# Two instructions in place of sixteen: GpSimd's splitting of the output weights, block by block

## The chip, the cores and the metric

The kernel runs on one core of one Trainium2 chip. What counts is the time of one execution on the device in microseconds (us), as a median over runs.

## The reference

Two layers of a diffusion backbone over 1024 latent tokens and 256 context tokens, with a model width of 1024. Each layer normalises, modulates, projects in, mixes the tokens, gates, projects out with a 1024 x 1024 matrix, normalises again and adds the result to its input. Layer 0 mixes with dense attention and with an RWKV scan side by side, layer 1 with windowed attention. Cut to what matters here:

```python
def _even_mixer(hx, hc, ..., w_in, w_out, ...):
    ...
    oa_x = _dense_attention(qx, jnp.concatenate([kx, kc], axis=1), jnp.concatenate([vx, vc], axis=1))
    ...
    out_x = jnp.concatenate([oa_x * jax.nn.silu(gax), ob_x * jax.nn.silu(gbx)], axis=-1) @ w_out

def _odd_mixer(hx, hc, ..., w_in, w_out, ...):
    ...
    ox = _window_attention(qx, kx, _heads(vx, C_KV_HEADS), kc, vc, sink)
    out_x = (ox * jax.nn.silu(gx)) @ w_out
```

## The kernel before

The program is a row of stages with a barrier of all engines between them: modulation, input projection, decay streams, the chunked scan, dense attention, closing of layer 0, then input projection, window attention and closing of layer 1. All data is float32; matmuls of a projection are done as three products of a high half and a low half. The high half of a weight is its value rounded to the type fp32r, the low half is what the rounding left.

The output projection's weight is split into these halves one stage early, in `attention`, on GpSimd (POOL), which has nothing else to do there but some memsets at the start. `prepare` hands over the weight `w` in device memory and the two targets `w_hi` and `w_lo`, each 128 partitions x 8 x 1024. The weight comes in four blocks of 256 columns (`BLK`), through one buffer `w_raw` of 128 x 8 x 256 (`KC` is 8). For each block POOL waits until the buffer is free (L1765), issues the load of 1 MB from its own queue (L1766), waits for it (L1767), rounds (L1769) and subtracts (L1772). The first block waits until the first result tile of attention is done (`out_done`, L1763). The next stage, `closing`, is the first to read `w_hi` and `w_lo`, on TensorE (PE).

Attention itself goes by units. A unit is one tile of 128 queries by one group of four heads. In dense attention there are 20 units, in window attention 32. PE works in steps, one tile of 128 keys each. In a step it computes the turned scores (L1920 to L1925), perhaps one piece of the plain scores (L1892 to L1901), whose largest value is wanted ahead of the exponential, and the products with V (L1939). VectorE (DVE) does for a unit, in this order in its queue:

- L1814, `highest`: one reduce over the score piece in PSUM for each piece, four or eight a unit. The scores have one buffer, so PE's next piece waits for this reduce (`topped`).
- `turn`, after the last piece: the negated maximum (L1824 in window attention; L1827, or L1829 and L1831, in dense attention), then L1833, which multiplies the identity by it into `shift`, 128 x 512, and in window attention L1838, `sd`. Here these instructions are called the unit's chain.
- L1850 and L1854, `finish`: the division by the row sums.

Two steps after a unit's last piece PE spreads `shift` over the partitions (L1906); ScalarE (ACT) copies it into QM (L1786), and computes the exponentials (L1782).

Of the kernel before, what the change touches and what calls it, by code (L numbers as in the profile page):

```python
# [14 lines left out]
F32 = mybir.dt.float32  # L15
F32R = mybir.dt.float32r
ALU = mybir.AluOpType
# [12 lines left out]
KC = D // P  # L30
# [1586 lines left out]
def attention(nc, name, qst, kst, vrows, consts, orows, ngroups, units, edge=None, sink=None, prepare=None):  # L1617
# [40 lines left out]
    with Stage(nc, name) as st:  # L1658
# [25 lines left out]
        if prepare:  # L1684
            w, w_hi, w_lo = prepare
            w_raw = st.sb("w_raw", [P, KC, BLK])
            w_in, w_high, w_low = st.sems("w_in", "w_high", "w_low")
# [13 lines left out]
        with nc.Block() as block:  # L1701
# [42 lines left out]
            @block.gpsimd  # L1744
            def _(pool):
                pool.wait_ge(loaded, 16 * NCONST)
                pool.tensor_copy(ones_r[:], ones[:]).then_inc(rounded, 1)
                pool.wait_ge(rounded, 1)
                if window:
                    pool.tensor_copy(eye[:], ident[:]).then_inc(rounded, 1)  # L1750
                    pool.wait_ge(rounded, 2)
                    pool.tensor_copy(masks[:], masks_raw[:]).then_inc(rounded, 1)
                    pool.wait_ge(rounded, 3)
                pool.memset(KL[HD:P].rearrange("p g n -> p (g n)").bitcast(F32), 0.0).then_inc(filled, 1)
                pool.wait_ge(filled, 1)
                pool.memset(KL[HD:HD + 1].rearrange("p g n -> p (g n)").bitcast(F32), 1.0).then_inc(filled, 1)
                pool.wait_ge(filled, 2)
                pool.memset(V[:, :, :, HD:HW], 1.0).then_inc(filled, 1)
                pool.wait_ge(filled, 3)
                for b in range(D // BLK if prepare else 0):  # L1760
                    cols = slice(b * BLK, (b + 1) * BLK)
                    if b == 0:
                        pool.wait_ge(out_done, 1)  # L1763
                    if b >= 1:
                        pool.wait_ge(w_low, b * KC)  # L1765
                    pool.dma_start(w_raw[:], w.rearrange("(k p) n -> p k n", p=P)[:, :, cols]).then_inc(w_in, 16)  # L1766
                    pool.wait_ge(w_in, b * 16 + 16)  # L1767
                    for k in range(KC):
                        pool.tensor_copy(w_hi[:, k, cols], w_raw[:, k]).then_inc(w_high, 1)  # L1769
                    for k in range(KC):  # L1770
                        pool.wait_ge(w_high, b * KC + k + 1)
                        pool.tensor_tensor(w_lo[:, k, cols], w_raw[:, k], w_hi[:, k, cols].bitcast(F32), ALU.subtract).then_inc(w_low, 1)  # L1772

            @block.scalar
            def _(act):
# [90 lines left out]
            def _(pe):  # L1866
# [10 lines left out]
                def measure(i, q):  # L1877
                    u, s, g = units[i], i % NSLOT, units[i]["group"]
                    r, x = q // spans[i], q % spans[i]
                    width = len(tiles_of[i]) * P // spans[i] // 2  # L1880
                    lhs = Q[:, s, r * P:(r + 1) * P]
                    if q == 0:
                        pe.wait_ge(k_in[g], 16)
                        pe.wait_ge(q_in[s], (i // NSLOT + 1) * 16)
                    if window:
                        kts = [kt for kt, _ in u["edges"]]
                        wide = len(kts) * P
                        step = (kts[-1] - kts[0]) if len(kts) > 1 else 1
                        edges = K[:, g].rearrange("p (t n) -> p t n", n=P)[:, kts[0]:kts[-1] + 1:step]
                        to = score[:, 0, 0:wide].rearrange("p (t n) -> p t n", n=P)  # L1890
                        which = [w for _, w in u["edges"]]
                        pe.matmul(to, lhs, edges, start=True, stop=False)  # L1892
                        pe.matmul(to, eye[:], masks[:, which[0]:which[-1] + 1], start=False, stop=True)
                        mid, ctx0 = u["plain"][0] * P, u["plain"][1] * P
                        pe.matmul(score[:, 0, wide:width], lhs, K[:, g, ctx0:ctx0 + width - wide], start=True, stop=True)
                        pe.matmul(score[:, 1, 0:P], lhs, K[:, g, mid:mid + P], start=True, stop=True)
                        last = pe.matmul(score[:, 1, P:width], lhs, K[:, g, ctx0 + width - wide:ctx0 + 2 * P], start=True, stop=True)  # L1897
                    else:
                        for b in range(2):
                            c0 = u["plain"][0] * P + (x * 2 + b) * width  # L1900
                            last = pe.matmul(score[:, b, 0:width], lhs, K[:, g, c0:c0 + width], start=True, stop=True)  # L1901
                    last.then_inc(scored, 1)
# [478 lines left out]
```

## Time and profile before

| what | value |
|---|---|
| median of three runs | 2652.66 us (2643.16 to 2656.72) |
| the profiled execution | 2652.66 us |
| its span, first to last instruction | 2650.9 us |
| mean granted TensorE clock | 0.907 of full speed |
| busy: PE, weight loads, DVE, ACT, POOL | 83%, 69%, 47%, 31%, 26% |
| instructions on POOL | 736 |

The busy share is the share of the span in which an engine executes an instruction, averaged over stages that have different limits. The granted clock is what the clock gate gave TensorE: 1.00 is 2.4 GHz and 0.50 is 1.2 GHz. A duration on DVE or POOL includes the time for which the instruction is held up after its start.

### The profile page before, as it was taken

To read this page: it belongs to the slowest core of one execution; us is meant where nothing else is said; L and a number is where in the kernel's file an instruction comes from. 1 tells how busy PE (TensorE), PEld (TensorE's weight loads), DVE (VectorE), ACT (ScalarE), POOL (GpSimd) and SP (SyncE) were. 2 spreads that over 40 slices of the span, in tenths; PEclk is the share of its full clock that TensorE was granted. 3 is DMA by queue.
4 is the path that set the end of the run, shared out by engine and by line. 5 is a ranking of instruction groups with operands and counts; after the bars stand their busy time and mean duration, and the time that the engine had idled before them with its cause. 6 is when DMAs were issued, how large, how long until landed. Compare 5 with 4: busy or idle time off the path is not lost. (4 is left out here: it accounts for less than half of the span.)

```text
span 2650.9 us, 59737 instructions
## 1 busy us (share of the span) xinstructions
PE 2188.2 (83%) x26094; PEld 1832.5 (69%) x26094; DVE 1256.8 (47%) x1692; ACT 825.7 (31%) x1393; POOL 694.9 (26%) x736
## 2 busy tenths in 40 slices
PE   4699999766558888888599998695799969999988
PEld 1588878622247777777488887574687758888866
DVE  1544553169725444454334442893546524444422
ACT  1311232155324444444123332221334302333321
POOL 0322463100023332323031000252357623200002
PEclk8799999877769999999779998797799978999989
DMA  6232333277632222221311110754344443211152
GB/s 219 93 108 85 94 96 105 62 257 278 252 108 80 63 85 62 87 70 38 85 64 48 41 33 30 226 162 161 117 110 105 120 116 109 65 56 48 38 196 88
DMA packets 232090, 282.38 MB, mean 107 GB/s; under 512 B 59796, under 2 KB 174676, under 8 KB 230804
## 3 DMA queue, kind: packets, MB, share of 16 engines
q1 hardware_dynamic: 204808, 194.28, 24.1%
q0 software_dynamic: 20688, 81.58, 9.1%
q8 instruction: 208, 3.41, 0.5%
q10 hardware_dynamic: 6336, 2.70, 0.4%
q14 instruction: 50, 0.41, 0.1%
HBM read 190.54 MB, written 87.95 MB: 105 GB/s over the span
## 5 line engine op out<-in xcount | busy, mean ns | idle before, releaser
L216 PE MATMUL in_acc<-in_hi,in_whi 128*128 128x512 f32 (+1 forms) x1024 | 392.2, 383 | 20.8 <-DVE in_lo L579 17.2
L216 PE MATMUL in_acc<-in_lo,in_whi 128*128 128x512 f32 (+1 forms) x1024 | 376.0, 367 | 0.0
L216 PE MATMUL in_acc<-in_hi,in_wlo 128*128 128x512 f32 (+1 forms) x1024 | 375.7, 367 | 0.0
L216 PEld LDWEIGHTS in_acc<-in_hi,in_whi 128*128 128x128 f32 x1024 | 196.2, 192 | 59.5 <-issue 28.3
L216 PEld LDWEIGHTS in_acc<-in_lo,in_whi 128*128 128x128 f32 x1024 | 196.6, 192 | 37.0 <-issue 7.2
L216 PEld LDWEIGHTS in_acc<-in_hi,in_wlo 128*128 128x128 f32 x1024 | 196.1, 191 | 31.8
L1814 DVE TENSOR_REDUCE dense_top<-dense_score 128x1 f32<-128x640 f32 (+1 forms) x144 | 112.3, 780 | 189.6 <-PE dense_score L1901 189.6
L1814 DVE TENSOR_REDUCE window_top<-window_score 128x1 f32<-128x640 f32 (+1 forms) x128 | 101.2, 791 | 190.5 <-PE window_score L1897 190.5
L1939 PEld LDWEIGHTS dense_outs<-dense_V,dense_p 128*128 128x128 f32 x1344 | 185.8, 205 | 5.0 <-ACT dense_p L1782 0.4
L1939 PE MATMUL dense_outs<-dense_V,dense_p 128*128 128x65 f32 x1344 | 182.0, 282 | 0.0
L1939 PE MATMUL window_outs<-window_V,window_p 128*128 128x65 f32 x1216 | 158.0, 274 | 0.2 <-ACT window_p L1782 0.2
L1939 PEld LDWEIGHTS window_outs<-window_V,window_p 128*128 128x128 f32 x1216 | 155.0, 195 | 4.0 <-ACT window_p L1782 0.6
L1468 PE MATMUL scan_wide<-scan_XT,scan_Y 64*64 64x64 f32 x3200 | 121.1, 224 | 24.1 <-issue 24.1
L1335 DVE TENSOR_TENSOR scan_X<-scan_X,scan_small 128x512 f32<-128x512 f32 x80 | 55.0, 687 | 180.9 <-PE scan_small L1463 179.7
L1782 ACT ACTIVATE dense_p<-dense_turned 128x512 f32<-128x512 f32 x168 | 96.6, 597 | 122.9 <-PE dense_turned L1925 122.4
L216 PE MATMUL close_acc<-w_hi,close_hi 128*128 128x512 f32 x288 | 117.6, 408 | 18.4 <-DVE close_lo L2187 18.4
L2113 POOL MEMSET close_eps<- 128x1 f32 x2 | 0.2, 104 | 496.7 <-POOLq L127 496.7
L1444 PE MATMUL scan_small<-scan_X,scan_off 64*64 64x64 f32 x3200 | 117.7, 225 | 8.2 <-issue 7.2
L1468 PEld LDWEIGHTS scan_wide<-scan_XT,scan_Y 64*64 64x64 f32 x3200 | 107.1, 136 | 24.7 <-issue 24.6
L1222 POOL TENSOR_TENSOR scan_off<-scan_LA,scan_lmask 128x512 f32<-128x512 f32 x100 | 124.0, 1275 | 0.0
L1213 POOL TENSOR_TENSOR scan_DG<-scan_LB,scan_lmask 128x512 f32<-128x512 f32 x20 | 25.3, 1265 | 364.3 <-ACT scan_LB L1249 364.3
L1444 PEld LDWEIGHTS scan_small<-scan_X,scan_off 64*64 64x64 f32 x3200 | 108.2, 140 | 14.0 <-issue 12.9
(256 smaller groups left out, 5038.6 us busy)
## 6 DMA issues: line engine op xcount, KB each, us to landing
streams<-decay_out POOLq DMA_DIRECT2D x8, 2560.0 KB, 13.1
scan_L<-streams SPq DMA_DIRECT2D x80, 256.0 KB, 3.6
decay_wm<-in_w_mod SPq DMA_DIRECT2D x16, 1024.0 KB
in_raw<-in_w_in_even SPq DMA_DIRECT2D x28, 512.0 KB, 3.7
in_raw<-in_w_in_odd SPq DMA_DIRECT2D x20, 512.0 KB, 3.9
close_ga<-gates SPq DMA_DIRECT2D x18, 512.0 KB, 4.5
modulation_w<-in_w_mod SPq DMA_DIRECT2D x4, 2048.0 KB, 15.4
gates<-in_outs POOLq DMA_DIRECT2D x32, 256.0 KB, 2.3
```

What stands on the lines that cost most here:

```text
L216: last = pe.matmul(out, a(k), b(k), start=(k == 0 and x == 0), stop=(k == n - 1 and x == 2))
L1213: pool.tensor_tensor(DG[:], LB[:], lmask[:, 0:1, :].to_broadcast([P, NU, HD]), ALU.mult).then_inc(diagonal, 1)
L1222: pool.tensor_tensor(off[s][:, k], triangles, lmask[:, k + 1:k + 2, :].to_broadcast([P, NU, HD]), ALU.mult).then_inc(off_done, 1)
L1335: dve.tensor_tensor(X[s][:], X[s][:], small[s][:], ALU.subtract).then_inc(x_less[s], 1)
L1444: return pe.matmul(small[s][half_of(1 - c), u, :], off[s][half_of(c), k, u, :], X[s][half_of(c), u, :], start=True, stop=True)
L1468: return pe.matmul(wide[s][half_of(1 - c), u, :], Y[s][half_of(1 - c), u, :], XT[j % 3][half_of(1 - c), u, :], start=True, stop=True)
L1782: act.activation(p[:, s % NP_], turned[s % NTURN][:], ACT.Exp, scale=SCALE).then_inc(expd, 1)
L1814: dve.tensor_reduce(top[:, i % NSLOT, x, r:r + 1], score[:, :, 0:width], AXS, ALU.max).then_inc(topped, 1)
L1939: last = pe.matmul(outs[i % 2][:, r * HW:(r + 1) * HW], p[:, s % NP_, r * P:(r + 1) * P], v, start=(k == 0 and r == 0), stop=(k == n - 1 a ...
L2113: pool.memset(eps[:, 0:1], EPS).then_inc(readied, 1)
```

## The change

Each block's eight casts of 256 columns become one cast of the whole block, and its eight subtractions one subtraction. The semaphores `w_high` and `w_low` count one for each block, not eight. The loads, the buffer and the order of the blocks stay.

```diff
                     if b >= 1:
-                        pool.wait_ge(w_low, b * KC)
+                        pool.wait_ge(w_low, b)
                     pool.dma_start(w_raw[:], w.rearrange("(k p) n -> p k n", p=P)[:, :, cols]).then_inc(w_in, 16)
                     pool.wait_ge(w_in, b * 16 + 16)
-                    for k in range(KC):
-                        pool.tensor_copy(w_hi[:, k, cols], w_raw[:, k]).then_inc(w_high, 1)
-                    for k in range(KC):
-                        pool.wait_ge(w_high, b * KC + k + 1)
-                        pool.tensor_tensor(w_lo[:, k, cols], w_raw[:, k], w_hi[:, k, cols].bitcast(F32), ALU.subtract).then_inc(w_low, 1)
+                    pool.tensor_copy(w_hi[:, :, cols], w_raw[:]).then_inc(w_high, 1)
+                    pool.wait_ge(w_high, b + 1)
+                    pool.tensor_tensor(w_lo[:, :, cols], w_raw[:], w_hi[:, :, cols].bitcast(F32), ALU.subtract).then_inc(w_low, 1)
```

## Rows read from the trace of the kernel before

**Rows 1.** Stretches: length, busy time (instructions) of each engine, granted clock, DMA share, GB/s

```profile
2218.00:2278.00 60.00, 54.38 (x396) 50.14 (x396) 29.14 (x56) 18.38 (x38) 36.88 (x67) 1.00 0.32 101
```

**Rows 2.** Waits in 1320 to 1690 us: who waited for whom, total, times, longest

```profile
POOL close_eps L2113 <- POOLq L127: 240.5, 1, 240.5
```

**Rows 3.** Timeline of POOL, dense attention: start, length, instruction, count

```profile
1355.14 2.80 POOL L1769 CAST w_hi<-dense_w_raw 128x256 fp32r<-128x256 f32 x8 [6.28 <-DMA dense_w_raw<-in_w_out_even]
1357.91 5.96 POOL L1772 TENSOR_TENSOR w_lo<-dense_w_raw,w_hi 128x256 fp32r<-128x256 f32 x8
...
1385.57 3.26 POOL L1769 CAST w_hi<-dense_w_raw 128x256 fp32r<-128x256 f32 x8 [5.50 <-DMA dense_w_raw<-in_w_out_even]
```

**Rows 4.** Timeline of POOL, window attention

```profile
2220.80 2.80 POOL L1769 CAST w_hi<-window_w_raw 128x256 fp32r<-128x256 f32 x8 [7.18 <-DMA window_w_raw<-in_w_out_odd]
2223.57 5.55 POOL L1772 TENSOR_TENSOR w_lo<-window_w_raw,w_hi 128x256 fp32r<-128x256 f32 x8
...
2235.99 2.80 POOL L1769 CAST w_hi<-window_w_raw 128x256 fp32r<-128x256 f32 x8 [5.63 <-DMA window_w_raw<-in_w_out_odd]
2238.75 6.00 POOL L1772 TENSOR_TENSOR w_lo<-window_w_raw,w_hi 128x256 fp32r<-128x256 f32 x8
...
2252.60 2.80 POOL L1769 CAST w_hi<-window_w_raw 128x256 fp32r<-128x256 f32 x8 [6.65 <-DMA window_w_raw<-in_w_out_odd]
2255.37 5.54 POOL L1772 TENSOR_TENSOR w_lo<-window_w_raw,w_hi 128x256 fp32r<-128x256 f32 x8
...
2267.72 2.81 POOL L1769 CAST w_hi<-window_w_raw 128x256 fp32r<-128x256 f32 x8 [5.62 <-DMA window_w_raw<-in_w_out_odd]
2270.49 5.98 POOL L1772 TENSOR_TENSOR w_lo<-window_w_raw,w_hi 128x256 fp32r<-128x256 f32 x8
```

**Rows 5.** Groups of POOL by form: busy us, mean ns of one, idle before

```profile
L472 POOL TENSOR_TENSOR in_work<-in_work,in_shift 128x1024 f32<-128x1024 f32 x20 | 47.9, 2394 | 76.9 <-DVE in_work L573 76.9
...
L503 POOL TENSOR_TENSOR in_work<-in_work,in_hu 128x512 f32<-128x512 f32 x30 | 38.7, 1291 | 7.5 <-DVE in_hu L614 7.5
...
L1752 POOL CAST window_masks<-window_masks_raw 128x256 fp32r<-128x256 f32 x1 | 0.4, 400 | 0.1
L1750 POOL CAST window_eye<-window_ident 128x128 fp32r<-128x128 f32 x1 | 0.3, 294 | 0.1
```

**Rows 6.** Timeline of DVE, dense attention

```profile
1359.36 0.66 DVE L1827 TENSOR_SCALAR dense_ntop<-dense_top 128x4 fp32r<-128x4 f32 x1
...
1387.03 0.33 DVE L1829 TENSOR_SCALAR dense_top<-dense_top 128x4 f32<-128x4 f32 x1
```

**Rows 7.** Timeline of DVE, window attention

```profile
2240.72 0.16 DVE L1824 SCALAR_TENSOR_TENSOR window_ntop<-window_top,window_nsinks_up 128x4 fp32r<-128x4 f32 x1
...
2251.66 0.16 DVE L1824 SCALAR_TENSOR_TENSOR window_ntop<-window_top,window_nsinks_up 128x4 fp32r<-128x4 f32 x1
...
2252.47 0.15 DVE L1838 TENSOR_TENSOR window_sd<-window_ntop,window_sinks_up 128x4 f32<-128x4 f32 x1
...
2262.22 0.16 DVE L1824 SCALAR_TENSOR_TENSOR window_ntop<-window_top,window_nsinks_up 128x4 fp32r<-128x4 f32 x1
...
2271.35 0.57 DVE L1824 SCALAR_TENSOR_TENSOR window_ntop<-window_top,window_nsinks_up 128x4 fp32r<-128x4 f32 x1
2271.96 1.19 DVE L1833 TENSOR_TENSOR window_shift<-window_ident,window_ntop 128x512 fp32r<-128x512 f32 x1
2273.07 0.68 DVE L1838 TENSOR_TENSOR window_sd<-window_ntop,window_sinks_up 128x4 f32<-128x4 f32 x1
```

**Rows 8.** Line L1833: count, shortest, median and longest in ns, first and last start

```profile
L1833 DVE TENSOR_TENSOR window_shift<-window_ident,window_ntop x32: 691/691/1191, 2180.8 to 2514.8; 128x512 fp32r<-128x512 f32 x32
```

**Rows 9.** Timeline of PE, window attention, at the only wait of this kind

```profile
2274.55 0.39 PE L1892 MATMUL window_score<-window_K,window_Q 128*128 128x256 f32 x1 [0.39 <-DVE window_top L1814]
```

**Rows 10.** Stretches of dense attention, columns as in rows 1

```profile
1440.00:1445.00 5.00, 3.61 (x24) 2.96 (x22) 1.42 (x4) 1.83 (x4) 0.00 (x0) 1.00 0.00 0
...
1445.50:1458.50 13.00, 12.08 (x48) 11.01 (x48) 3.76 (x6) 2.27 (x4) 0.00 (x0) 0.50 0.00 1
...
1470.00:1530.00 60.00, 55.70 (x395) 51.29 (x394) 28.29 (x48) 21.21 (x37) 0.00 (x0) 1.00 0.12 36
```

## The prediction

> **What bounds the kernel now.** The changed lines run only inside the two attention stages, so I look there first. The table of stretches shows what limits window attention while POOL splits the weight: PE is busy for 54.38 of 60 us, DVE for 29.14, POOL for 36.88 [rows 1]. PE sets the pace, and a microsecond in which PE waits is lost. Dense attention has the same picture with POOL idle: PE 55.70 of 60 [rows 10].
>
> Next I ask who waits for POOL. In the list of waits of dense attention POOL's own next work comes after 240.5 us of idling at the stage's end [rows 2]; the halves are read only in the stage after that. So whatever POOL saves here is not on the path. A first answer would be: no change.
>
> The third view is the timeline of DVE beside that of POOL, because a change of instruction length can act on a neighbour. L1833 takes 691 ns in the median but at most 1191 [rows 8], and the three instructions of the chain at 2271.35 took 0.57, 1.19 and 0.68 us [rows 7], where 0.16, 0.69 and 0.15 are usual [rows 7, 8]. All three lie within POOL's subtractions of 2270.49 to 2276.47 [rows 4]. The chain at 2251.66, when POOL was waiting for its load, has no such excess. So DVE is held up by a POOL instruction, each time by no more than about 0.5 us, which fits a wait until the POOL instruction under way (5.5 us over 8 is 0.7 us) has ended. In dense attention L1827 at 1359.36 took 0.66 [rows 6], also within POOL's subtractions [rows 3].
>
> What does such a wait cost PE? The chain at 2271.35 was held for 0.41 + 0.50 + 0.53 = 1.44 us, and shortly after it PE waited 0.39 us for DVE's maximum at 2274.55 [rows 9]. Hence a chain has about 1.44 - 0.39 = 1.05 us of slack, and what exceeds it stalls PE one for one.
>
> **The change part by part.**
>
> *Cast.* 294 ns for 128 columns, 400 for 256 [rows 5]: 0.83 ns a column. For the block's 8 x 256 = 2048 columns that is 400 + 1792 x 0.83 = 1.9 us in place of 2.80. The upper bound is the 2.80 of now, if nothing is saved.
>
> *Subtraction.* 1291 ns for 512 columns, 2394 for 1024 [rows 5]: 2.15 ns a column, and 2394 + 1024 x 2.15 = 4.6 us for 2048, in place of 5.5 to 6.0 [rows 4]. The upper bound again is the present time.
> Seen by itself: the Trainium skill, GPSIMD Engine Reference, section on elementwise work side by side, gives 4497 ns for a two-input add of 2048 columns. By it each subtraction would end 0.1 us sooner, and each wait below would be 0.1 us shorter, 0.2 us in the sum.
>
> A block then takes 6.5 us and not 8.3 to 8.8. POOL has about 2 us less work a block, eight blocks in all, some 16 us. That is hidden by the idling of [rows 2] and worth 0. The four loads of each stage start up to 6 us sooner; POOL issues the same DMAs from the same queue, no other instruction stands behind them, and DVE does not read what they bring. I cost that at 0, too.
>
> *The longer instruction.* POOL is now inside one instruction for 4.6 us at a stretch, where it had boundaries every 0.7 us at which DVE could get in. If DVE waits for the end of the instruction under way, a chain that falls into a subtraction waits up to 4.6 us, not 0.5. I place the new subtractions by keeping POOL's gaps between blocks (load and waits). Window attention [rows 4]:
> - block 0: cast from 2220.80, end 2227.3.
> - block 1: the gap is 2235.99 - 2229.12 = 6.9, so cast from 2234.2, subtraction 2236.1 to 2240.7. The chain at 2240.72 [rows 7] just escapes.
> - block 2: gap 2252.60 - 2244.75 = 7.85, cast from 2248.55, subtraction 2250.45 to 2255.05. The chain at 2251.66 is caught and waits 3.4 us; PE stalls 3.4 - 1.05 = 2.3 us.
> - block 3: gap 2267.72 - 2260.91 = 6.8, cast from 2261.9, subtraction 2263.8 to 2268.4. The chain of 2262.22, now 2.3 later at 2264.5, is caught and waits 3.9; PE stalls 2.8 us.
> - the chain of 2271.35 is free, and its 0.39 us of PE stall goes away.
>
> Sum for window attention: 2.3 + 2.8 - 0.4 = +4.7 us.
>
> Dense attention [rows 3, 6]: block 0's subtraction would lie at 1357.0 to 1361.6, the chain at 1359.36 waits 2.3 us, 1.2 over the slack. Its present two waits cost PE nothing, and PE's steps are longer there, so I take 0 and keep 1.2 for the range. Block 2 starts two savings of about 2 us sooner than 1385.57: subtraction 1383.4 to 1388.0, so the chain at 1387.03 waits 1.0, within the slack: 0.
>
> The sum is +4.7 us on the profiled execution of 2652.66, which is also the median: 2657.
>
> How firm is it? A wait is known from the rows only up to about 0.5 us; beyond that I assume that the wait grows with the POOL instruction. From below, the wait could stay at half a microsecond: then the sum is 0, or -0.4. From above, all eight subtractions could catch a chain at their start: 8 x (4.6 - 1.05) = +28 us. Chains come every 10.9 us (2240.72, 2251.66) and POOL subtracts for 4.6 us in about 14, so a chain is caught one time in three. I take my placed value, since the two catches in window attention have 1.2 us and 0.7 us of room before they would be missed.
> Seen by itself: the Trainium skill, SBUF — State Buffer, section on who interferes with whom, speaks against this change. It says that DVE and GpSimd share one pair of ports as an exclusive lock, held for the whole instruction by whichever came first, and that a DVE instruction with two SBUF inputs contends with a GpSimd instruction that reads SBUF. The short waits agree; no row yet shows a long one. By the rule the sum is the +4.7 above, by a wait capped at what the rows show it is -0.4.
>
> **The rivals.**
>
> *R1, nothing happens.* The wait does not grow, or the chains miss the subtractions because the loads land at other moments, or the merged instructions are no quicker than the eight they replace (the gain per instruction is not real; the engine would then only show other boundaries). For it: the catches hang on placements good to half a microsecond. Against it: every chain inside POOL work shows an excess now. Time: 2652 to 2653.
>
> *R2, the clock falls (slower).* PE at 1440 to 1445 was busy for only 3.61 of 5 us, and from 1445.5 to 1458.5 the granted clock was 0.50 (1.2 GHz) [rows 10]. In that stretch PE issued 48 matmuls in 13 us, 3.7 per us, against 395 in 60 us, 6.6 per us, at 1.00: it cost 13 x (1 - 3.7/6.6) = 5.7 us. A stall of 2.3 or 2.8 us leaves PE as idle or idler than before that fall. One such stretch added gives 2657.4 + 5.7 = 2663, two give 2669. It decides the sign beyond my bound from the second stretch on, or with one that lasts over 20 us. Against it: window attention ran at 1.00 throughout [rows 1], with margin unknown.
>
> *R3, faster.* The low stretches of dense attention move, and some fall away, as the waits of DVE shift. Each is worth 5.7 us by the same row; three would be needed to show. What speaks for it is only that the present runs differ by 13 us among themselves. Time: below 2639.
>
> **How the numbers follow.** What a measurement of this kernel can tell from no change is about 0.5%, 13.3 us. Chances: my forecast, one to three chains caught and no low stretch added, 2657 (2653 to 2662), 0.50. R1, 2652, 0.22. R2 with one added stretch, 2663, 0.12; with two or more, over 2666, 0.12. R3, 0.04. So faster 0.04, same 0.50 + 0.22 + 0.12 = 0.84, slower 0.12. The range leaves out the last two of these, 0.16: its lower end is the lowest of the runs before, 2643, for R1; its upper end is the lower part of the case with two stretches, 2669.
>
> **What would show it.** L1769 and L1772 with 4 instructions each a stage, at about 1.9 and 4.6 us, and POOL's blocks 6.5 us long: the change does what it says. An instruction of the chain (L1824, L1833, L1838, L1827, L1829, L1831) with 2 us or more that ends when POOL's does: the long wait is real. PE waits of 2 to 3 us for L1814 just after it: the slack is as I read it. L1814 and L1854, which read PSUM, should keep their lengths. Window attention at clock 1.00 until its end: R2 is out. I am wrong if long waits are there and PE does not stall (more slack than 1.05), or if many more chains are caught than two, for instance because each stall shifts the next chain into the next subtraction; or if the stages end later with no wait of this kind in them.

## The result, and the profile after

| | before | after |
|---|---|---|
| median of 20 runs | 2653.49 us | 2676.55 us |
| lowest and highest | 2636.52, 2686.54 | 2654.41, 2709.42 |
| ratio, with its 95% interval | | 1.0086 (1.0062 to 1.0109) |

The ratios here and below leave out disturbed executions, the medians do not, so a ratio can differ a little from that of the two medians. The change makes the kernel slower by 0.86%, about 23 us. The prediction said 2657 with a range up to 2669.

The profiled execution of the changed kernel took 2659.85 us (span 2658.1), only 7 us more than that of before; it is not a typical one, and below it is seen why. Lines from L1773 on have moved up by two: L1831 is what L1833 was.

First, what the change was to do. The groups on the two weight halves, with shortest, median and longest duration in ns:

```profile
L1768 POOL CAST w_hi<-dense_w_raw x4: 1880/1885/1887, 1352.8 to 1395.6; 128x2048 fp32r<-128x2048 f32 x4
L1770 POOL TENSOR_TENSOR w_lo<-dense_w_raw,w_hi x4: 4522/4562/4577, 1354.8 to 1397.5; 128x2048 fp32r<-128x2048 f32 x4
L1768 POOL CAST w_hi<-window_w_raw x4: 1886/1887/1889, 2202.6 to 2242.3; 128x2048 fp32r<-128x2048 f32 x4
L1770 POOL TENSOR_TENSOR w_lo<-window_w_raw,w_hi x4: 4542/4547/4562, 2204.6 to 2244.2; 128x2048 fp32r<-128x2048 f32 x4
```

1.9 and 4.5 us, as worked out from [rows 5]. POOL's busy time falls from 694.9 to 678.2 us. The saving is real, and it is nowhere on the path. Second, the timelines of POOL and DVE in window attention, blocks 2 and 3 (compare [rows 4, 7]):

```profile
2231.17 4.54 POOL L1770 TENSOR_TENSOR w_lo<-window_w_raw,w_hi 128x2048 fp32r<-128x2048 f32 x1
...
2244.25 4.54 POOL L1770 TENSOR_TENSOR w_lo<-window_w_raw,w_hi 128x2048 fp32r<-128x2048 f32 x1
```

```profile
2234.19 1.54 DVE L1822 SCALAR_TENSOR_TENSOR window_ntop<-window_top,window_nsinks_up 128x4 fp32r<-128x4 f32 x1
...
2244.74 4.07 DVE L1822 SCALAR_TENSOR_TENSOR window_ntop<-window_top,window_nsinks_up 128x4 fp32r<-128x4 f32 x1
2248.84 0.69 DVE L1831 TENSOR_TENSOR window_shift<-window_ident,window_ntop 128x512 fp32r<-128x512 f32 x1
```

An instruction on four columns, 0.16 us by itself, takes 4.07 us. It ends at 2248.81, POOL's subtraction at 2248.79. The one at 2234.19 ends at 2235.73, POOL's at 2235.71. So DVE waits for the end of the POOL instruction, here for up to 3.9 us. The reduces over PSUM in between keep their length: L1812 takes 0.827 us at most, as L1814 did before.

Third, PE behind it. Its timeline, with the wait ahead of the instruction in brackets, and then the stretches (columns as in [rows 1]) of what follows, and of the whole of window attention after and before:

```profile
2250.26 0.42 PE L1890 MATMUL window_score<-window_K,window_Q 128*128 128x128 f32 x1 [2.73 <-DVE window_top L1812]
```

```profile
2250.20:2301.20 51.00, 48.32 (x191) 44.66 (x192) 13.46 (x30) 9.82 (x19) 0.00 (x0) 0.50 0.10 31
...
2154.70:2535.60 380.90, 344.28 (x2248) 317.15 (x2248) 157.04 (x317) 111.19 (x217) 35.65 (x15) 0.89 0.23 65
```

```profile
2172.10:2528.20 356.10, 321.79 (x2247) 296.52 (x2248) 154.20 (x317) 110.88 (x217) 43.59 (x71) 0.95 0.25 70
```

PE waits 2.73 us once, and from about 2250 to 2301 the granted clock is 0.50 (1.2 GHz), where before it was 1.00 at the same work. The stage with the same 2248 weight loads takes 380.9 us in place of 356.1: 24.8 more, of which the wait itself is 2.7. The rest, 22.1 us, is the 51 us at half clock, 0.43 us for each. That is about the loss of a median run. In this one execution dense attention won some back, as it happened to have less time at half clock (329.2 us for the stage against 343.8, next section), which is why its total is only 7 us up.

This share can be read from the totals too. Each execution comes with its mean granted clock, so its time at half clock is 2 x (1 - clock) x time. Of two executions of the kernel before, one (2637.92 us, clock 0.917) had 438 us of it, the other (2674.19, 0.902) 524: 36 us of time for 86 us at half clock, 0.42 each. The changed kernel has a median clock of 0.901 over 45 executions, 530 us at half clock; the kernel before 0.910 over 35, 476 us. 54 us more at 0.42 to 0.44 each are 23 to 24 us, the size of the result.

### The profile page after: what moved, and what is told of

Read it like the earlier page. It is cut to its first block and busy times, and to the rows that moved or that the text cites. A ratio compares the mean times of both kernels' runs of the same rounds, so it can differ in the third digit from the quotient of the medians.

```text
span 2658.1 us, 59625 instructions
## 1 busy us (share of the span) xinstructions
PE 2186.1 (82%) x26094; PEld 1834.1 (69%) x26094; DVE 1257.7 (47%) x1692; ACT 825.6 (31%) x1393; POOL 678.2 (26%) x624
## 5 line engine op out<-in xcount | busy, mean ns | idle before, releaser
L1812 DVE TENSOR_REDUCE window_top<-window_score 128x1 f32<-128x640 f32 (+1 forms) x128 | 101.2, 791 | 211.9 <-PE window_score L1895 211.9
L1812 DVE TENSOR_REDUCE dense_top<-dense_score 128x1 f32<-128x640 f32 (+1 forms) x144 | 112.3, 780 | 175.7 <-PE dense_score L1899 175.7
L1937 PEld LDWEIGHTS dense_outs<-dense_V,dense_p 128*128 128x128 f32 x1344 | 176.9, 197 | 4.8 <-ACT dense_p L1780 0.4
L1937 PE MATMUL dense_outs<-dense_V,dense_p 128*128 128x65 f32 x1344 | 173.9, 274 | 0.0
L1937 PEld LDWEIGHTS window_outs<-window_V,window_p 128*128 128x128 f32 x1216 | 166.3, 207 | 4.3 <-ACT window_p L1780 0.6
L1937 PE MATMUL window_outs<-window_V,window_p 128*128 128x65 f32 x1216 | 168.8, 286 | 0.2 <-ACT window_p L1780 0.2
```

The costliest lines, as they stand in the source:

```text
L1812: dve.tensor_reduce(top[:, i % NSLOT, x, r:r + 1], score[:, :, 0:width], AXS, ALU.max).then_inc(topped, 1)
L1937: last = pe.matmul(outs[i % 2][:, r * HW:(r + 1) * HW], p[:, s % NP_, r * P:(r + 1) * P], v, start=(k == 0 and r == 0), stop=(k == n - 1 a ...
```

## The experiments

T is the theory that came out of the profile: a chain on DVE waits for the end of a long POOL instruction, PE stalls, the granted clock falls behind the stall and stays low. All results in one table. The kernel before ran beside each group (median 2653.9, 2651.6, 2662.6 and 2657.3 us for e1 to e4, e6 to e9, e5 with e10 and e11, and e12; at half clock 476, 473, 485 and 478 us), and each ratio is to its own group. The last column is the median time at half clock, worked out as above. e6 has only 4 executions, e9 9, e5 10, the others 12 each and the changed kernel 45.

| run | what differs from the kernel before | ratio (95% interval) | median us | at half clock |
|---|---|---|---|---|
| after | all merged | 1.0086 (1.0062 to 1.0109) | 2676.6 | 530 |
| e1 | merged in dense only | 1.0021 (0.9994 to 1.0047) | 2657.9 | 473 |
| e2 | merged in window only | 1.0076 (1.0045 to 1.0107) | 2675.7 | 519 |
| e3 | casts merged | 1.0013 (0.9978 to 1.0047) | 2663.2 | 492 |
| e4 | subtractions merged | 1.0056 (1.0021 to 1.0091) | 2675.8 | 527 |
| e5 | two parts in one | 1.0074 (1.0029 to 1.0119) | 2678.3 | 523 |
| e6 | four parts in one | 1.0085 (1.0057 to 1.0113) | 2671.9 | 508 |
| e7 | all merged, started behind a chain | 0.996 (0.9928 to 0.9992) | 2643.3 | 457 |
| e8 | DVE held 4.15 us at unit 12 | 1.0048 (1.0016 to 1.0080) | 2660.9 | 495 |
| e9 | DVE held 1.08 us at unit 12 | 1.0009 (0.9978 to 1.0040) | 2653.9 | 483 |
| e10 | DVE held 4.15 us at unit 7 | 1.0077 (1.0038 to 1.0115) | 2684.6 | 529 |
| e11 | eight parts, started behind a chain | 0.998 (0.9949 to 1.0011) | 2658.8 | 473 |
| e12 | DVE held 2.15 us at unit 7 | 1.0055 (1.0021 to 1.0089) | 2674.1 | 513 |

### e1 and e2: one stage at a time

Both, and e3 to e6, use the lines below, with CK parts to a cast and SK to a subtraction. The loop of the subtractions, changed in the same way with SK, is left out.

```diff
+                    CK, SK = (1 if window else KC), (1 if window else KC)    # e1; e2: KC if window else 1
-                        pool.wait_ge(w_low, b * KC)
+                        pool.wait_ge(w_low, b * (KC // SK))
-                    for k in range(KC):
-                        pool.tensor_copy(w_hi[:, k, cols], w_raw[:, k]).then_inc(w_high, 1)
+                    for k in range(0, KC, CK):
+                        pool.tensor_copy(w_hi[:, k:k + CK, cols], w_raw[:, k:k + CK]).then_inc(w_high, 1)
```

> Merged instructions in dense attention alone; window attention as before. Theory T (a chain on DVE waits for the long subtraction, PE stalls, and the granted clock falls behind the stall and stays low for tens of us): the cost depends on which stage's chains are caught and how near PE is to a fall of the clock there. Dense attention has falls already in the kernel before and its chains come only every 14 us, so less than half of the +23 us of the full change: 0 to +8 us. Rival U (the cost is in both stages alike, by the length of the instructions): half, about +11 us. Rival N (the difference is chance of where the low stretches fall, nothing of the change): 0, and the other stage alone 0 too.

> Merged instructions in window attention alone. T: most of the cost, +12 to +23 us, and in the profile at least one chain instruction of over 2 us that ends with POOL's subtraction, a PE wait of over 1 us right behind it and a stretch at clock 0.50 that begins there. U: about +11 us. N: 0.

Nearly all of the cost is in window attention, and the theory of chance falls. Equal shares (U) would be 11 us or 0.41% for each stage: that lies below e2's interval, though still inside e1's. The profile of e2 shows the same picture at another instruction of the chain, L1839 (`sd`, 0.15 us by itself); timelines of DVE and of PE, and the stretch behind:

```profile
2257.08 4.47 DVE L1839 TENSOR_TENSOR window_sd<-window_ntop,window_sinks_up 128x4 f32<-128x4 f32 x1
```

```profile
2262.20 0.47 PE L1893 MATMUL window_score<-window_K,window_Q 128*128 128x128 f32 x1 [3.56 <-DVE window_top L1815]
```

```profile
2261.40:2309.00 47.60, 44.17 (x175) 40.80 (x176) 12.94 (x28) 9.82 (x19) 0.12 (x1) 0.50 0.11 33
...
2165.70:2545.60 379.90, 342.39 (x2247) 315.49 (x2248) 159.88 (x317) 111.19 (x217) 35.63 (x15) 0.89 0.23 65
```

In e1 the longest instructions of a dense chain took 1.63 and 2.27 us, held up by 1.46 and 1.58; PE's wait behind the second was 1.35 us where 0.92 is usual, and no stretch at 0.50 began there.

### e3 and e4: casts or subtractions alone

```diff
+                    CK, SK = KC, 1    # e3;  e4: 1, KC
```

> Casts merged in both stages (1.9 us), subtractions left at eight a block. T: a wait is at most 1.9 us, 0.8 us over the slack of 1.05 us, and a chain is seldom caught: within 4 us of the kernel before. If the merged cast too brings the clock down by such small stalls, +5 us or more. N: 0.

> Subtractions merged in both stages (4.5 us), casts left at eight a block. T: nearly the full cost, +15 to +23 us, with waits of up to 4.5 us on the chain. U: about 4.5/6.4 of the full cost, +16 us, so it does not tell T from U, but from a theory by which the casts matter. N: 0.

The casts alone cost nothing that can be told from no change, the subtractions at least 0.2%; 0.56%, about 15 us, is the lower end of what I expected. In the profile of e4 `sd` took 4.48 us, PE waited 3.54 us, and 33.5 us at half clock followed. e3's interval leaves room for up to +0.47%, and its profile has one catch that counts: in dense attention a merged cast stretched `shift` from 0.69 to 2.39 us, PE waited 1.47 us, and 17.1 us at half clock began there. The 2.27 us in e1 were also a merged cast's doing, with nearly the same wait of PE and no fall. So a merged cast can do the same harm; how often it does is not shown.

### e5 and e6: two and four parts in one instruction

```diff
+                    CK, SK = 2, 2    # e5;  e6: 4, 4
```

> Two of a block's eight parts in one instruction, in both stages: casts of 0.6 us, subtractions of 1.3 us. A chain of three instructions can be caught by each of them in turn, as the kernel before shows at 0.5 us each: up to 3 x 1.2 = 3.5 us for a chain, 2.4 over the slack. If what counts is the longest single wait, under the slack: +0 to +3 us. If what counts is the sum over the chain: stalls of up to 2 us, and +8 to +20 us as with four parts in one.

> Four of a block's eight parts in one instruction, both stages: casts of about 1.1 us, subtractions of about 2.35. A wait is at most 2.35 us, a stall at most 1.3 us. T: if such a stall brings the clock down as the longer ones do, about half of the full change's cost, +8 to +15 us; if not, under +4 us. Theory N2 (the cost follows the number of caught chains, whatever the length): the full +22 us.

Here my expectation for e6 was a cost of about half. It is the full one, and so is e5's. The timelines of DVE and PE in e6 show why:

```profile
2259.54 0.80 DVE L1825 SCALAR_TENSOR_TENSOR window_ntop<-window_top,window_nsinks_up 128x4 fp32r<-128x4 f32 x1
2260.38 2.83 DVE L1834 TENSOR_TENSOR window_shift<-window_ident,window_ntop 128x512 fp32r<-128x512 f32 x1
2263.13 2.29 DVE L1839 TENSOR_TENSOR window_sd<-window_ntop,window_sinks_up 128x4 f32<-128x4 f32 x1
```

```profile
2266.08 0.48 PE L1893 MATMUL window_score<-window_K,window_Q 128*128 128x128 f32 x1 [3.75 <-DVE window_top L1815]
```

The chain has three instructions, and each waits anew for the POOL instruction then under way: 0.64 + 2.14 + 2.14 = 4.9 us together, more than one merged subtraction could hold it. What counts is the sum over the chain: one chain earlier in the same profile only `shift` was held, by 2.14 us, PE's wait behind it was 1.18 us where 0.92 is usual, and the clock stayed at 1.00. In the kernel before, the same three waits add up to 1.44 us [rows 7, 8], 0.39 over the slack. N2 foretold the full cost too; against it, the kernel before catches two chains of window attention in its profile, for half a microsecond at a time, and the clock does not fall behind them. The profiled execution of e5 had no such stretch in window attention (clock 0.95 over the stage, as before): its longest held chain lost 1.00 + 1.08 us, PE waited 1.12 us where 0.78 to 0.92 is usual, and the clock stayed at 1.00. Its ten executions together show the cost, so its mechanism is inferred from e6, not seen.

### e7 and e11: the same work, started behind a chain

```diff
                     pool.wait_ge(w_in, b * 16 + 16)
+                    pool.wait_ge(sink_d, 4 + 2 * b) if window else pool.wait_ge(shifted, 4 + b)
```

e7 is the changed kernel with this line, e11 the kernel before with it. POOL starts a block when DVE has just finished a chain, and the block ends before the next.

> The full change, merged instructions in both stages, but POOL starts a block only behind a chain of DVE (it waits for the count of sink_d in window attention, of shifted in dense attention), so that the 6.5 us of a block end ahead of the next chain. Theory T (long waits of a chain, then a fall of the clock): no chain is caught, the cost goes: within 4 us of the kernel before, median about 2654, time at half clock near the 476 us of the kernel before. Rival L (the merged instructions cost by themselves, through the loads or POOL's own work): still about +22 us, 2676.

> The kernel before, eight casts and eight subtractions a block, but POOL starts each block behind a chain, as in the run with the merged instructions behind a chain. If the gain of that run over the kernel before (ratio 0.996) comes from chains that are no longer held up at all, the same ratio, 0.994 to 0.998. If it comes from the merged instructions, 1.000.

e7 takes the whole cost away and is faster than the kernel before, with 1.0 outside its interval. In its profile no instruction of a chain is held up in either stage (`shift` takes 0.69 us at most). Its POOL timeline, and both attention stages:

```profile
2238.41 1.88 POOL L1769 CAST w_hi<-window_w_raw 128x2048 fp32r<-128x2048 f32 x1 [13.79 <-DVE window_sd L1837]
2240.38 4.54 POOL L1771 TENSOR_TENSOR w_lo<-window_w_raw,w_hi 128x2048 fp32r<-128x2048 f32 x1
```

```profile
1304.40:1623.00 318.60, 289.09 (x1988) 262.48 (x1988) 141.98 (x238) 108.01 (x188) 30.87 (x14) 0.96 0.18 50
2147.20:2502.70 355.50, 321.57 (x2248) 296.69 (x2248) 151.83 (x317) 110.88 (x217) 36.01 (x15) 0.95 0.25 70
```

POOL stands idle 13.8 us, for its load and then for the chain (5.6 to 7.2 us where it waits for the load alone [rows 4]), at no cost, and the merged instructions are as long as in the changed kernel. Dense attention takes 318.6 us here, against these rows of the changed kernel and of the kernel before:

```profile
1300.90:1630.10 329.20, 299.70 (x1987) 272.10 (x1988) 143.47 (x238) 108.15 (x188) 30.91 (x14) 0.93 0.17 49
```

```profile
1302.50:1646.30 343.80, 314.23 (x1987) 285.19 (x1988) 144.46 (x238) 108.45 (x188) 39.64 (x70) 0.88 0.16 46
```

Dense attention varies by 25 us, all of it in PE's busy time for the same matmuls. e9 and e10, which run the dense attention of the kernel before unchanged, took 332.3 and 325.4 us for it at clocks of 0.92 and 0.94. So a part of its low stretches comes and goes from one execution to the next, and one profile says little about it. e11's interval holds both 1.0 and e7's ratio: whether the gain of e7 needs the merged instructions stays open.

### e8, e9, e10, e12: a stall without POOL

The kernel before, with one extra reduce on DVE that reads one operand in SBUF, ahead of the chain of one unit of window attention.

```diff
                     dve.wait_ge(topped, first_piece[i + 1])
+                    HOLDS = {12: 30}    # e9: {12: 7}; e10: {7: 30}; e12: {7: 15}
+                    if window and i in HOLDS:
+                        dve.tensor_reduce(hold[:], ident[:, None, :].to_broadcast([P, HOLDS[i], P]), AXS, ALU.max).then_inc(held, 1)
+                        dve.wait_ge(held, sum(j <= i for j in HOLDS))
```

> The kernel before, POOL untouched, with one extra reduce on DVE of about 4.2 us ahead of the chain of unit 12 of window attention, where POOL is idle. It stands for one caught chain. T: PE waits 4.2 - 1.05 = 3.1 us once, the granted clock falls to 0.50 behind it and stays there for 30 to 50 us, each microsecond at half clock costing 0.44: 3 + 0.44 x 40 = about +20 us in most executions. Rival D (only the stall itself costs, the clock is not moved by one stall): +3 us.

> The same extra reduce at the same place, of about 1.1 us: no longer than the slack I read from the kernel before. T: PE waits under 0.3 us for it, no fall of the clock there, time as before within 5 us. If slack or fall begins earlier, a PE wait of about 1 us shows, and a stretch at 0.50 behind it.

> The extra reduce of 4.15 us on DVE, this time ahead of the chain of unit 7 and not 12: the place in window attention where the merged kernels had their stall (the chain near 2245 to 2260 us of the span). POOL is as in the kernel before. Theory P (how long the clock stays low depends on the place: on the work of PE behind the stall): a stretch at 0.50 of 34 to 51 us as in the merged kernels, and +3 us + 0.44 x 45 us = about +20 us. Rival Q (one stall always gives a short stretch, as the 13.7 us behind unit 12; the long stretches of the merged kernels need several stalls in a row): about +9 us, as with unit 12.

> The extra reduce ahead of the chain of unit 7, now of 15 x 128 columns, about 2.15 us: by the slack of 1.05 us a PE stall of 1.1 us. If a stall must be about as long as those of the merged kernels (2.7 to 3.8 us) to bring the clock down there, +1 us and no stretch at 0.50 behind it. If the place is so near a fall that a small stall does it, as pairs and fours of parts suggest, a long stretch again and +8 to +20 us.

e10 gives the full cost of the change with one delayed chain and POOL as before. e8 gives 0.48%, less than I expected, and e9, a hold of 1.08 us behind which PE's wait was the usual 0.92, gives nothing. e12 is the telling one; DVE, PE, and the stretches before, behind and after:

```profile
2269.32 2.15 DVE L1823 TENSOR_REDUCE window_hold<-window_ident 128x1 f32<-128x1920 f32 x1
```

```profile
2273.12 0.33 PE L1898 MATMUL window_score<-window_K,window_Q 128*128 128x128 f32 x1 [1.01 <-DVE window_top L1816]
```

```profile
2220.00:2270.00 50.00, 46.47 (x341) 43.26 (x340) 23.45 (x44) 16.94 (x33) 28.91 (x52) 1.00 0.40 116
2270.00:2320.00 50.00, 45.45 (x233) 41.66 (x231) 18.37 (x39) 11.74 (x24) 8.30 (x16) 0.69 0.19 57
2320.00:2370.00 50.00, 46.47 (x343) 43.28 (x342) 22.68 (x47) 15.82 (x31) 0.00 (x0) 1.00 0.16 50
```

A PE wait of 1.01 us was followed by a clock of 0.69 over 50 us, 31 us of them at 0.50; the rest of the stage, after its first 20 us, ran at 1.00. The stall itself is worth 0.04% of the time; the run is 0.55% slower. In the profile of e8 the wait was 3.31 us and only 13 us at half clock followed:

```profile
2320.60:2333.60 13.00, 11.86 (x48) 11.09 (x48) 3.41 (x8) 3.67 (x7) 0.00 (x0) 0.50 0.13 41
```

So the length of the low stretch does not follow the length of the stall. That it follows the place (unit 7 worse than unit 12) fits the medians, but the two intervals overlap, and in the one profile of e10 the stretch behind the stall (a wait of 3.38 us) was 13.7 us as well, while 64.8 us at half clock lay over the start of the stage, where the kernel before has 34 and 14 us. Place or chance stays open, and so does why a stretch lasts as long as it does.

That the stall brings the fall about is seen best in all fourteen profiles together. From 55 us into window attention on, the seven without an additional PE wait of 1 us (before, e1, e3, e5, e7, e9, e11) ran at 1.00 to its end. The seven with one (after, e2, e4, e6, e8, e10, e12) each have one stretch at 0.50, and it begins within 1.5 us of the end of that wait. In dense attention the tie is looser: behind waits of 1.35 us (e1) and 1.44 us (e10) no stretch began, behind one of 1.47 us (e3) one did, and the kernel before has stretches there with no such wait ahead of them.

## Why the prediction was wrong, by its steps

- *The durations held.* 1.9 and 4.6 us against 1.89 and 4.52 to 4.58; POOL's saving 16 us against 694.9 - 678.2 = 16.7. Worth nothing, as said.
- *DVE waits for the end of the whole instruction: right.* That the wait would grow from the half microsecond of the rows with the length was an extrapolation; an instruction of 0.15 us that took 4.48 us (e4) shows it. So the Trainium skill's rule (SBUF — State Buffer, who interferes with whom), an exclusive lock held for the whole instruction, agrees with this case, and the rival of a capped wait is out.
- *Which chains are caught: roughly right.* In window attention I placed two catches with waits of 3.4 and 3.9 us; the profile has 1.4 and 3.9. In dense attention 2.3 us was 1.5, and cost PE nothing, as taken. That one wait fits to the tenth is luck: in e2, with the same instructions in this stage, the last chain was held by 4.7 us in all, most of it at `sd`.
- *The slack: right for the chains that stalled PE, too small for others.* 1.05 us was read from one wait of 0.39. Where a long wait showed ahead of a score piece, the runs give 3.91 - 2.73 = 1.18 (after), 4.74 - 3.56 = 1.18 (e2), 4.9 - 3.75 = 1.2 (e6), 2.15 - 1.01 = 1.14 (e12). But chains held by 1.38 us (after) and 1.67 us (e2) left PE's next wait at its usual 0.78, and at unit 12 a hold of 4.15 us raised it from 0.92 to 3.31, which leaves 1.8. So the stalls of window attention were not 2.3 and 2.8 us but 0 and 2.73, and the sum of +4.7 came to little more than half.
- *The step that failed is the clock.* The sum of +4.7 us leaves it as it was, and R2, which prices its fall, took 5.7 us for a stretch of 13 us, read from one fall in dense attention [rows 10], and set the sign only from the second stretch on, with 0.24 in all. Measured behind a caught chain in window attention: 51 us at half clock (after), 47.6 (e2), 33.5 (e4), 47.5 (e6), at 0.43 us each some 14 to 22 us. One stretch is enough. The mechanism of R2 happened as written, with its price per microsecond (1 - 3.7/6.6 = 0.44) right and its length two and a half to four times too small.
- *The evidence against R2 was misread.* I took the 60 us of [rows 1] for the whole stage. They are at 1.00, but window attention before began at half clock (0.95 over the stage), and [rows 10] show one of the shorter falls of dense attention. The trace has one of 27.3 us there, and in the 6.5 us ahead of it PE had waited no more than 0.52 us at a time:

```profile
1356.50:1383.80 27.30, 25.86 (x100) 23.53 (x99) 8.14 (x12) 6.14 (x11) 17.45 (x31) 0.50 0.27 95
...
2172.10:2210.00 37.90, 29.80 (x113) 25.64 (x114) 12.14 (x21) 5.65 (x10) 5.80 (x3) 0.55 0.67 149
```

  Priced by the first of these, one stretch is 12 us. The "margin unknown" was the thing to ask for: e12 shows that one microsecond of PE waiting more than usual can use it up. The chance of 0.12 for slower should have been much larger, since I expected two stalls of over 2 us in that stage.
- *The forecast of "no change" for the total was wrong* for the same reason; the 2.7 us of stalls alone would have stayed below what can be told.

## What to carry to other kernels

An engine with nothing on the critical path can still do harm with one long instruction: DVE instructions with two operands in SBUF, and here also a tensor_scalar on four columns, wait for GpSimd's to end (1.68 us in place of 0.17 in the changed kernel). Before merging instructions on GpSimd, look at who gets in between them, and add up the waits over all dependent instructions behind each other, not the longest. If a long instruction is wanted, start it on a semaphore that says that the neighbour's sensitive part has just ended; e7 did that with one line and was 0.4% faster than the kernel before (0.1 to 0.7%), and by the two ratios 1.3% faster than the changed one. And where TensorE runs at full clock with regular short waits, price a stall by the stretch at half clock that may follow, not by its own length.

## What was unexpected of the hardware

- A single additional PE wait of 1.01 us was followed by 31 us at 1.2 GHz, waits of 2.7 to 3.8 us by 33 to 51 us, but those of 3.31 and 3.38 us by 13 us only. Waits of 1.12 us (e5) and 1.18 us (e6) in the place of the usual 0.78 to 0.92 were followed by no fall. In the stretches behind these stalls PE was busy for 91 to 97% of the time (48.32 of 51.00, 11.86 of 13.00, 32.56 of 33.50 us).
- Executions of one and the same kernel differ by 1.4% (2637.92 to 2674.19 us) with its mean granted clock (0.917 to 0.902), at 0.42 us for each microsecond at half clock. One profile of this kernel therefore does not show a change of 1%; the changed kernel's own profile is 17 us below its median.
